# A two-block network with long convolutions: the last projection chunk of the Hyena mixer moved behind an inverse transform

## What is computed

```python
def bidir_long_conv(u, hf, hb, skip):
    L = u.shape[1]
    kfull = jnp.concatenate([hf, jnp.zeros_like(hf[:1]), hb[:0:-1]], axis=0)
    K = jnp.fft.rfft(kfull, n=2 * L, axis=0)
    U = jnp.fft.rfft(u, n=2 * L, axis=1)
    y = jnp.fft.irfft(U * K[None], n=2 * L, axis=1)[:, :L]
    return y + u * skip

def hyena_mixer(h, w_in, conv_w, conv_b, ..., skip, w_out):
    z = short_conv(h @ w_in, conv_w, conv_b)
    x1, x2, v = jnp.split(z, 3, axis=-1)
    hf, hb = hyena_filters(...)
    y = v
    for n, gate in enumerate((x1, x2)):
        y = gate * bidir_long_conv(y, hf[:, n], hb[:, n], skip[n])
    return y @ w_out
```

## Time and profile before

| | us |
|---|---|
| median of 3 runs | 3176.22 |
| lowest, highest | 3174.80, 3176.24 |
| the profiled execution, its own time | 3173.9 |
| its span, first to last instruction | 3172.0 |
| TensorE busy in it | 3134.4 (99%) |
| VectorE busy | 1982.0 (62%) |
| ScalarE busy | 1224.7 (39%) |
| GpSimd busy | 596.0 (19%) |

### The profile page before, as it was taken

One profiled execution on the slowest core, in us unless ns is written; L12 is line 12 of the kernel. 1 busy time (PEld: TensorE's weight loads), 2 busy tenths in 40 slices (PEclk: granted clock), 3 DMA queues, 4 the chain that ended last, 5 costly groups with the idle time before them and its releaser, 6 DMA issues.

```text
span 3172.0 us, 36265 instructions
## 1 busy us (share of the span) xinstructions
PE 3134.4 (99%) x14870; PEld 2547.1 (80%) x14870; DVE 1982.0 (62%) x2666; ACT 1224.7 (39%) x1645; POOL 596.0 (19%) x463
## 2 busy tenths in 40 slices
PE   9999999999999999999999999999999999999998
PEld 7877788888888788888888866778888888888887
DVE  7555657566666566577656567766555589964333
ACT  4234442333432334422244355644343353442222
POOL 1000000000100010699981010002433001010001
PEclk9999999999999999999999999999999999999999
DMA  3222243454222222355432000023333322322221
GB/s 129 81 93 81 86 146 133 169 190 185 93 93 87 76 94 92 142 188 202 181 113 100 27 29 28 28 87 116 130 113 127 132 105 82 114 86 93 106 94 67
DMA packets 55621, 342.40 MB, mean 108 GB/s; under 512 B 5984, under 2 KB 7840, under 8 KB 18208
## 3 DMA queue, kind: packets, MB, share of 16 engines
q1 hardware_dynamic: 54080, 337.46, 29.4%
q10 hardware_dynamic: 1376, 2.62, 0.2%
HBM read 327.47 MB, written 12.58 MB: 107 GB/s over the span
## 4 chain that ended last, share of the span: by engine, by line
PE 87%; DVE 8%; ACT 4%; issue 1%; DMA 0%; POOLq 0%; POOL 0%; ACTq 0%; DVEq 0%
PE PS L264 86%; DVE wl L273 2%; DVE FA L281 1%; ACT PB L270 1%; DVE UL L273 1%; PE PS L267 1%; ACT SC L270 1%; ACT UH L270 1%; DVE SC L273 1%; DVE SC L281 1%; DVE PB L273 1%; DVE PS L273 0%; DVE ST L293 0%; ACT FA L270 0%; ACT wh L270 0%
## 5 line engine op out<-in xcount | busy, mean ns | idle before, releaser
L264 PE MATMUL PS<-UH,wh 128*128 128x512 f32 (+1 forms) x2120 | 837.6, 395 | 4.7 <-DVE UL L273 1.8
L264 PE MATMUL PS<-UH,wl 128*128 128x512 f32 (+1 forms) x2120 | 824.2, 389 | 0.0
L264 PE MATMUL PS<-UL,wh 128*128 128x512 f32 (+1 forms) x2120 | 823.9, 389 | 0.0
L273 DVE TENSOR_TENSOR wl<-raw,wh 128x2048 fp32r<-128x2048 f32 (+2 forms) x255 | 562.2, 2206 | 386.0 <-ACT wh L270 385.9
L264 PE MATMUL PS<-RH,wh 128*128 128x512 f32 (+2 forms) x1640 | 644.9, 393 | 1.7 <-DVE RL L281 0.9
L264 PE MATMUL PS<-RH,wl 128*128 128x512 f32 (+2 forms) x1640 | 638.6, 389 | 0.0
L264 PE MATMUL PS<-RL,wh 128*128 128x512 f32 (+2 forms) x1640 | 638.4, 389 | 0.0
L270 ACT ACTIVATE wh<-raw 128x2048 fp32r<-128x2048 f32 (+2 forms) x255 | 452.5, 1780 | 241.4 <-DMA raw<-in_wall 174.5
L264 PEld LDWEIGHTS PS<-UH,wh 128*128 128x128 f32 x2120 | 400.4, 189 | 109.6 <-issue 19.2
L264 PEld LDWEIGHTS PS<-UL,wh 128*128 128x128 f32 x2120 | 400.4, 189 | 83.1 <-issue 3.8
L264 PEld LDWEIGHTS PS<-UH,wl 128*128 128x128 f32 x2120 | 400.1, 189 | 82.9
(11 more groups left out here) (218 smaller groups left out, 3107.3 us busy)
## 6 DMA issues: line engine op xcount, KB each, us to landing
raw<-in_wall SPq DMA_DIRECT2D x224, 1024.0 KB, 4.8
FA<-in_wmod SPq DMA_DIRECT2D x48, 1024.0 KB, 4.9
raw<-in_wall SPq DMA_DIRECT2D x29, 512.0 KB, 3.5
kspec<-FA SPq DMA_DIRECT2D x8, 1024.0 KB, 6.5
FA<-kspec SPq DMA_DIRECT2D x8, 1024.0 KB, 6.9
PB<-in_window SPq DMA_DIRECT2D x16, 256.0 KB, 4.4
Hs<-in_xT ACTq DMA_DIRECT2D x4, 512.0 KB, 8.4
FA<-in_w SPq DMA_DIRECT2D x4, 512.0 KB, 5.6
```

The lines of the kernel that those rows point to most:

```text
L264: return self.put(self.eng and self.eng.matmul(out, w, x, start=start, stop=stop, skip_group_check=True))
L273: return self.put(self.eng and self.eng.tensor_tensor(out, a, b, op))
```

## The change

Three moves by hand in the lists of three engines, nothing else. On TensorE `chunk(11)` goes behind `spectra(3, 1)` and `inverse(3, 0)`. On ScalarE `butterfly(3, 1)` goes ahead of `chunk(11)`, `w_hi(("ho", 0))` and `mixed(0)`. On VectorE `products(3, 1)` goes ahead of `chunk(11)`, `w_lo(("ho", 0))` and `mixed(0)`. The lists of GpSimd and SyncE and the number of instructions stay.

```diff
@@ tensor_program, hyena
             inverse(2, 1)
             chunk(10)
-            chunk(11)
             spectra(3, 1)
             inverse(3, 0)
+            chunk(11)
             for j in range(2):
                 out_part(j, range(4))
             inverse(3, 1, of=high)
@@ scalar_program, hyena
             chunk(10, (3, 0))
+            butterfly(3, 1)
             chunk(11)
             w_hi(("ho", 0))
             mixed(0)
-            butterfly(3, 1)
             products(3, 1)
@@ vector_program, hyena
             chunk(10, (3, 0))
+            products(3, 1)
             chunk(11)
             w_lo(("ho", 0))
             mixed(0)
-            products(3, 1)
             products_low(3, 1)
             gated(3, 1)
```

## The result

The changed kernel is slower: 3184.53 us median of 9 runs (3181.54 to 3189.03) against 3175.57 us for before (9 runs, 3172.32 to 3178.74), +8.96 us. The ratio is 1.0032 with a 95% interval of 1.0024 to 1.0041, that is +7.6 to +13 us, clear of the 0.2% named above. The forecast was 3186.9 us, that is +10.65.

What follows compares the result with a forecast made beforehand. TensorE, 99% busy, was taken as the bound, with VectorE's 23.6 us ahead of the last inverse. 3.6 + 7.9 - 2.7 - 1.55 = 7.25, plus 1.7 twice for the clock, gave +10.65 us: 3186.9, range 3181.1 to 3190.5.

Steps and rivals of the forecast that it cites:

- the 0.2% named above: Limit of what a measurement of this kernel can tell from no change, 6.35 us; chance 0.88 of being slower by more.
- VectorE's chain of block and products: VectorE's gapless 9.72 us of w_lo, taps and RL tiles plus 13.90 us of products(3, 1), ahead of the UL tile.
- The first wait: TensorE ahead of spectra(3, 1), waiting for z1 from VectorE's second PB addition: 3.6 us that chunk 11 hid before.
- VectorE's hold at `gated(3, 0)`: VectorE, in the earlier products, waits for tiles of inverse(3, 0): 0.3 us, or 2.0 with a drop of the clock.
- The second wait: TensorE ahead of out_part, behind chunk 11, waiting for RL tile 0 from VectorE: 7.9 us.
- the floor: Wait left at out_part even with VectorE free, since RH must wait for chunk 11's last sum: some 4.8 us.
- The gain: At inverse(3, 1), the old wait of 2.7 us and its slow clock of 1.55 us go: 4.2 us.
- The rest of the output product: Behind inverse(3, 1), the last RH and RL tiles are paced as before: costed at nothing, a few tenths if cover fails.
- The clock: Each new TensorE wait is followed by a stretch at reduced clock: 1.7 us each, bounds 0 and 1.7, up to 3.4.
- The total: The local sum of +10.65 us added to the median of 3176.2 us: 3186.9 us.
- Faster: Rival: early products free the last inverse and the block hides under chunk 11, winning 4.2 us; chance 0.04.
- The margin of ScalarE's chain: ScalarE's w_hi at 2751.1 is used by VectorE at 2752.5, 1.4 us; lateness was part of a slower rival, chance 0.08.

Runs made afterwards that it cites:

- e2: Changed kernel with one 2.2 us VectorE operation moved from products(3, 0) to behind products_low(3, 0), so z1 comes sooner: 3184.69 us, ratio 1.0033.
- e3: Changed kernel with mixed(0) moved ahead of w_lo of ho 1 and chunk 11's taps on VectorE, and ahead of w_hi on ScalarE: 3178.71 us, ratio 1.0012.
- e6: Kernel before with VectorE's four taps of chunk 11 moved from ahead of mixed(0) to between the second and third tile of gated(3, 1): 3172.83 us, ratio 0.9996.
- e1: Changed kernel with TensorE's list put back as before, the VectorE and ScalarE moves kept: 3191.01 us, ratio 1.0053.
- e9: Kernel before with chunk 11's VectorE taps split: first tile's between the two w_lo, second tile's behind products_low(3, 1): 3174.53 us, ratio 0.9994.
- e7: Changed kernel with filler matmuls on TensorE, 13 in the first wait and 32 in the second: 3183.72 us, ratio 1.0025.
- e8: The changed kernel itself, run and traced again beside the one with filler matmuls: 3183.22 us, ratio 1.0030.
- e5: Changed kernel with z1 sooner, TensorE's inverse(3, 1) ahead of out_part, RL ahead of the taps and ScalarE reordered: 3175.21 us, ratio 1.0002.
- e4: Kernel before with the four RL tiles of mixed(0) made by GpSimd instead of VectorE: 3175.32 us, ratio 1.0005.

## Why the prediction was right

**What bounds.** VectorE's chain of block and products, 23.6 us, was named as what TensorE waits for. e2, e3 and e6 show it: shift VectorE's work, and a wait of TensorE changes with it, by 1.9 to 4.9 us; shift TensorE alone (e1) and VectorE stands still too.

**The first wait.** Forecast 3.6 us from start to start, measured 3.49 (chunk 10 starts at 2709.88 and takes 10.9 us, the spectra start at 2724.28; 3.33 in the trace's count), released by the second PB addition. Right.

**VectorE's hold at `gated(3, 0)`.** Forecast 0.3 us without a drop of the clock, 2.0 with one; measured 1.07 + 0.69 = 1.76. Right.

**The second wait.** Forecast 7.9, measured 7.80 from start to start (7.64). Right in size and in cause; e3 splits it into 4.9 us of work that could stand elsewhere and a floor of 2.8. The forecast put the floor at 4.8 us, because it kept ScalarE's `w_hi` of 1.8 us ahead of RH, which e3 moved too.

**The gain.** The wait ahead of the last inverse and its slow clock went, 4.2 us: that inverse takes 5.75 us (2768.57 to 2774.32), its UL tiles having long been made. The prediction put the whole 1.55 us of it to the clock. e6 and e9 show that about half would have stayed at full clock, because UL tiles made 0.60 us apart hold an inverse at 6.5 us; the sum is right since both causes went. The rest of the output product, costed at nothing, takes 32.67 us in both kernels.

**The clock.** Forecast 1.7 us for each wait. Measured: spectra 7.22 instead of 5.44 (1.78), `out_part` 12.61 instead of 10.9 (1.70); e7 takes both away. The sum 3.49 + 7.80 + 1.78 + 1.70 - 4.23 is 10.54, and the local time says 10.55. So close an agreement holds some luck, in two places.

The first is the price of the second drop. The prediction put 3.4 us on a drop that lasts twice as long. It did last twice as long, 6.8 us, but half of it lay in the wait, where it costs nothing. Where it ends isn't fixed: `out_part` takes 1.7 us over 10.9 in the changed kernel, 1.9 in its second trace (e8), 2.0 in e1 and 2.7 in e2.

The second is whether a wait has a drop at all. That a wait just over 3 us brings one was the weakest step; in the two traces of the changed kernel it came each time, and in e3. Among waits of 2 to 3 us it can't be told from the length. In this part 2.52, 2.23 and 2.08 us were followed by a drop and the 2.78 us of e3 were not. At the wait near 2652 us, which no kernel touches, the 2.77 us of e9 were followed by one, and 2.01 (e8), 2.38 (e5), 2.40 (e4), 2.60 (e2) and 2.87 us (e1) were not. Behind the waits of 1 to 2 us at these places there was none.

**The total.** 8.96 instead of 10.65 us. The profiled executions are 7.8 us apart, of which the local part is +10.55; 2.8 us the other way come from elsewhere, where the kernels do not differ. Counted by the number of the matmul, the changed kernel loses 1.1 us at a drop near 54 us that lasts longer and 0.5 at the longer wait near 2652, and gains 1.6, 0.8 and 1.3 us near 904, 1726 and 3160 us, where only before has a drop; smaller shifts make up the rest. The step that was off is the last: adding a local sum to the median as if the rest stood still to a microsecond. The interval of +7.6 to +13 us covers the sum. (The top of the stated range adds up to 3190.2 and not 3190.5, which changes nothing.)

**The rivals.** "Faster" fell at the point that was named, the first RL tile: it comes 7.8 us after TensorE could use it. The margin of ScalarE's chain was there: its `w_hi` ended at 2751.51 and VectorE used it at 2752.93, and the first RH tile was made by 2752.0, ahead of RL at 2755.13.

## What to carry to other kernels

When two engines work through hand-written lists and one of them has no idle time in a stretch, moving a stage earlier on it only moves another later: write down for each tile when it is asked for and sort the busy engine's list by that, then move the consumer's list in the same order. Here the same move with the consumer's list changed as well and RL put ahead of the taps (e5) costs 1.8 us by the local time and nothing that the median can tell. Judge a change of a few microseconds in a kernel of three milliseconds by a stretch of the trace that begins ahead of the change and ends behind it, and use the total only to see that nothing large moved elsewhere.

## What the runs showed of the hardware

GpSimd and VectorE slowed each other when both read two operands from SBUF (e4: VectorE's 128x2048 subtraction took 3.38 us instead of 2.28, and GpSimd took 8.03 us for four tiles of 128x512, where one takes 1.29 us elsewhere in the same trace), and VectorE was not slowed when one of its operands came from PSUM (1.40 us for two, as before). Whether a wait of TensorE between 2 and 3 us is followed by a stretch at 1.2 GHz differs from case to case: 2.08, 2.23, 2.52 and 2.77 us were, 2.01, 2.38, 2.40, 2.60, 2.78 and 2.87 us were not. The stage behind it does not always lose the same: 1.55 to 1.8 us behind the waits of 2.08, 2.52 and 3.3 us, and 1.7 to 2.7 us behind those of 7.6 to 18.5 us, where the low clock begins inside the wait. Matmuls issued into the waits for nothing but to keep TensorE busy (e7) kept the granted clock at 1.00 behind both.
